# Attention of the second block's layers: values in column strips, outputs summed turned in PSUM, paired scores of the second tile in 64-row tiles

## The chip, the core and the metric

The kernel runs on one core of one Trainium2 chip. All data are fp32. The metric is the device time of one execution in microseconds: three runs of the kernel before gave a median of 1697.09 us (1696.93 to 1698.31).

## The reference

Two transformer blocks in a row on 256 tokens of 1024 channels. The first block (FFN, token mixer, FFN) isn't touched. The second has two layers, and each begins with a mixer of two attentions, whose outputs stand side by side ahead of the output product:

```python
for l in range(DEPTH_2):                       # 2 layers
    h = x @ w_in[l]
    cq, ckv, kr, nq, kc, vc, ks, vs, kw, vw, gl = jnp.split(h, split_at, axis=-1)
    o_a = mla_mixer(cq, ckv, kr, ...)          # 8 heads, 64 value columns each, causal
    o_b = nsa_mixer(nq, kc, vc, ks, vs, kw, vw, gl, ...)
    mix = jnp.concatenate([o_a, o_b], axis=-1) @ w_out[l]
    x = layer_norm(DEEPNORM_ALPHA * x + mix, ln1_g[l], ln1_b[l])
    ...                                        # memory attention, conv FFN
# nsa_mixer, for a block of 128 queries, 8 heads in 2 groups of 4 that share keys and values:
#   o_c: softmax over 15 compressed keys;  o_s: selected keys;  o_w: window keys
    return gi[..., 0:1] * o_c + gi[..., 1:2] * o_s + gi[..., 2:3] * o_w
```

With 256 tokens the selection and the window take in every earlier key, so o_s and o_w are two causal attentions with their own keys and values. `gi` are sigmoid gates, one for each token, head and branch.

## The kernel before

Each engine has its own program, written out by hand; the engines meet only through semaphores, so each engine's order is the order of the code. An attention is a list of units (`UNITS_2`), and a unit is a pair of heads (index `s`) for one tile of 128 queries. The kinds in question are K (all eight heads on the compressed keys), S (selected), W (window) and M (latent attention, `mla_mixer`). A tile has four units each of S, W and M, numbered `n`. In tile 0 a unit has 128 keys, in tile 1 it has 256. The order is K of tile 0, K of tile 1, then for each tile S0, W0, S1, W1, S2, W2, S3, W3, M0 to M3: 26 units.

A unit goes through a pipeline, with unit j at its scores while older units are behind:
- TensorE `scores(j)` (L1190): a 128x128 product for each head, into one half of `PS` (L1187). The keys of S and W are 64 channels in 128 rows, padded with zeros.
- VectorE `logits(j)` (L2357): adds the bias, takes the row maximum, and negates it (L2360).
- ScalarE `exps(j)` (L1692): exponential with row sums.
- TensorE `turn(j-2)` (L1206): transposes the probabilities, two blocks of 128 in tile 0, four in tile 1.
- ScalarE `out_of_psum(j-2)` (L1702): copies them into `PTS`, which has two buffers. Unit j's copy waits until the values of unit j-2 are done (`values_ready`, L1699). In each step of ScalarE's program this copy stands ahead of `exps(j)`.
- TensorE `value(j-3)` (L1232): the transposed probabilities are the weights (128 columns), the values move (64 columns), the outputs have tokens in the partitions.
- VectorE `output(j-3)`: reciprocal of the sums (L2403), for S and W times the gate (L2413), and scales the output out of PSUM into `O1`, S and W added onto what is there (L2419); M is written (L2421), K too, over 512 columns (L2408).

The M unit's bias is the causal mask alone. For K, `logits` is a memset and three small steps (L2338 to L2346), and `mid` masks the probabilities and sums them (L2371 to L2375). `mid(j)` on VectorE, between logits and output, does something only for kinds with `mid` set: here K.

A fp32 matmul appears as two passes in the trace, a transpose as one. Between the first steps stand four pieces of the memory values' product (L1538, eight passes of 512 columns each; TensorE's table `between`, L1556).

Behind the attention `shared_product` multiplies by `w_out` (L844). It needs the mix turned, channels in the partitions, in `XT`. TensorE turns `O1` in four batches of four transposes (L1116), two for each tile, and ScalarE copies each batch out (L1603, L1609). The first product blocks need only tile 0; later ones need sums of weights and of both tiles' activations, which VectorE makes after the attention (`weight_sums` L2191 to L2203, `act_sums` L2217 to L2223).

## Time and profile before

| what | value |
|---|---|
| median of three runs | 1697.09 us |
| profiled execution | 1696.81 us, its span 1694.9 us |
| TensorE busy (matmul) | 1665.5 us, 98% |
| VectorE busy | 1223.2 us, 72% |
| ScalarE busy | 352.5 us, 21% |
| chain that ended last | PE 90%, DVE 5% |

The span is what the profile covers; the device time is about 1.9 us longer. In the rows PE is TensorE's matmuls, PEld its weight loads, DVE is VectorE, ACT is ScalarE. The layers' attention stands at 831 to 892 us (layer 0) and again 481 us later (layer 1). A matmul's busy time includes the tail of its pipeline, so passes overlap in the rows; what one costs the next is read from the distance of the starts.

### The profile page before, as it was taken

What the parts mean: (1) busy time and instruction counts of PE and PEld (TensorE: products, weight loads), DVE (VectorE), ACT (ScalarE), POOL (GpSimd) and SP (SyncE); (2) the same over time, 40 slices, a digit from 0 to 9 for tenths busy, and PEclk for the clock granted to TensorE, in tenths of its full rate; (3) what the DMA queues carried; (4) which work ended last, traced back from release to release, by engine and by line L of the source; (5) the groups of instructions that cost most, each with busy time, mean ns of one, the idle gap of its engine ahead of it and who ended that gap; (6) DMA issues with size and microseconds to landing.
All of it is one profiled execution on the core that took longest, in us unless ns stands there. A gap on an engine that the chain in (4) does not pass through costs nothing.

```text
span 1694.9 us, 22817 instructions
## 1 busy us (share of the span) xinstructions
PE 1665.5 (98%) x8726; PEld 1281.4 (76%) x8726; DVE 1223.2 (72%) x2230; ACT 352.5 (21%) x893; POOL 212.7 (13%) x139
## 2 busy tenths in 40 slices
PE   7999999999999999999999999999999999999998
PEld 6887488877847886477784969994687767699953
DVE  6777467976787777573376778996844685789995
ACT  2111000034511111112270212220012531222210
POOL 1222211121021212211001000002120000000021
PEclk9999999999999999999999999999999999999999
DMA  9685454524176555346513536444447206265440
GB/s 320 194 230 177 146 199 162 175 80 149 51 232 213 160 164 184 124 145 178 207 51 131 155 125 194 156 170 153 158 121 252 100 1 224 71 226 177 150 173 25
DMA packets 163755, 267.07 MB, mean 158 GB/s; under 512 B 4279, under 2 KB 106477, under 8 KB 163519
## 3 DMA queue, kind: packets, MB, share of 16 engines
q1 hardware_dynamic: 157902, 248.66, 43.8%
q0 software_dynamic: 5008, 15.91, 3.3%
q8 instruction: 70, 1.15, 0.3%
q10 hardware_dynamic: 736, 1.05, 0.3%
q14 instruction: 39, 0.31, 0.1%
HBM read 262.52 MB, written 2.03 MB: 156 GB/s over the span
## 4 chain that ended last, share of the span: by engine, by line
PE 90%; DVE 5%; DVEq 2%; issue 1%; ACT 1%; DMA 1%; SPq 0%; ACTq 0%
PE psum L1017 19%; PE psum L886 16%; PE psum L1065 13%; PE psum L952 12%; PE psum L844 7%; PE psum L1275 4%; PE psum L1481 3%; PE psum L1538 3%; PE psum L1190 3%; PE psum L1116 3%; PE psum L1232 2%; PE psum L825 2%; PE psum L1104 2%; PE psum L1206 1%; PE psum L1221 1%
## 5 line engine op out<-in xcount | busy, mean ns | idle before, releaser
L695 POOL TENSOR_TENSOR work<-ring,work 128x1024 f32<-128x1024 f32 (+2 forms) x59 | 147.4, 2499 | 791.5 <-DVE work L2199 791.5
L2191 DVE TENSOR_TENSOR work<-ring 128x1024 f32<-128x1024 f32 (+2 forms) x102 | 122.0, 1196 | 83.3 <-PE psum L1065 74.3
L1065 PE MATMUL psum<-ring,work 128*128 128x512 f32 x352 | 160.8, 592 | 0.0
L2195 DVE TENSOR_TENSOR ring<-ring 128x1024 f32<-128x1024 f32 (+2 forms) x104 | 131.7, 1267 | 7.7
L2199 DVE TENSOR_TENSOR work<-ring 128x1024 f32<-128x1024 f32 (+2 forms) x102 | 122.6, 1202 | 7.6
L1065 PEld LDWEIGHTS psum<-ring,work 128*128 128x128 f32 x352 | 66.4, 190 | 81.1 <-issue 79.9
L1065 PE MATMUL psum<-work 128*128 128x512 f32 x264 | 122.5, 592 | 0.0
L1017 PE MATMUL psum<-x_t,work 128*128 128x128 f32 x832 | 101.4, 275 | 0.0
L1017 PE MATMUL psum<-work,ring 128*128 128x128 f32 x832 | 101.4, 275 | 0.0
L1017 PE MATMUL psum<-x_t,ring 128*128 128x128 f32 x832 | 97.4, 275 | 1.6 <-ACT x_t L1610 1.6
L1017 PEld LDWEIGHTS psum<-x_t,work 128*128 128x128 f32 x832 | 97.1, 192 | 0.0
L1017 PEld LDWEIGHTS psum<-work,ring 128*128 128x128 f32 x832 | 97.1, 192 | 0.0
L1017 PEld LDWEIGHTS psum<-x_t,ring 128*128 128x128 f32 x832 | 95.0, 192 | 2.4 <-issue 2.4
L1065 PEld LDWEIGHTS psum<-work 128*128 128x128 f32 x264 | 49.7, 190 | 62.0 <-issue 60.3
L2823 DVE SCALAR_TENSOR_TENSOR work<-work 128x254 f32<-128x254 f32 (+1 forms) x176 | 83.5, 526 | 3.3
L886 PE MATMUL psum<-ring,work 128*128 128x256 f32 x352 | 83.2, 379 | 0.0
L886 PE MATMUL psum<-ring,x_t 128*128 128x256 f32 x352 | 81.7, 386 | 1.5 <-DMA ring<-in_ffn_w_gate_dram 1.3
L886 PE MATMUL psum<-work,x_t 128*128 128x256 f32 x352 | 82.9, 379 | 0.0
L1190 PE MATMUL psum<-work 128*128 128x256 f32 (+2 forms) x384 | 79.5, 338 | 0.3 <-DVE stat L2360 0.3
L886 PEld LDWEIGHTS psum<-ring,x_t 128*128 128x128 f32 x352 | 67.9, 194 | 12.2 <-DMA ring<-in_ffn_w_gate_dram 2.4
L1692 ACT ACTIVATE work<-work,stat 128x256 f32<-128x256 f32 (+1 forms) x136 | 61.6, 453 | 66.5 <-DVE stat L2360 65.6
L886 PEld LDWEIGHTS psum<-ring,work 128*128 128x128 f32 x352 | 66.9, 190 | 9.1
(304 smaller groups left out, 2865.6 us busy)
## 6 DMA issues: line engine op xcount, KB each, us to landing
ring<-in_ffn_w_up_dram SPq DMA_DIRECT2D x66, 1024.0 KB, 7.9
ring<-in_w_in_dram SPq DMA_DIRECT2D x21, 2048.0 KB, 7.9
ring<-in_ffn_w_down_dram SPq DMA_DIRECT2D x20, 2048.0 KB, 7.8
ring<-in_ffn_w_gate_dram SPq DMA_DIRECT2D x22, 1024.0 KB, 5.7
ring<-in_xa_wkv_dram SPq DMA_DIRECT2D x8, 2048.0 KB, 9.5
ring<-in_w_out_dram SPq DMA_DIRECT2D x6, 2048.0 KB, 10.9
ring<-in_xa_wq_dram SPq DMA_DIRECT2D x4, 2048.0 KB, 7.9
ring<-in_xa_wo_dram SPq DMA_DIRECT2D x4, 2048.0 KB, 11.3
```

The costliest lines, as they stand in the source:

```text
L695: nc.gpsimd.tensor_tensor(t4, quarters(n, chunks, pitch)[2], t2, ALU.subtract).then_inc(fourth_ready, 1)
L844: last = mm(share_bank(p), acts[p][:, q, :], rhs[:, i, :], start=(q == 0), stop=(q == KD // 2 - 1))
L886: last = mm(corners(j)[p], acts[p][:, i, :], rhs[:, i, :], start=(i == 0), stop=(i == KD // 2 - 1))
L952: last = mm(row_corners(j)[p][:, 0:pitch // 2], acts[p][:, i, :], rhs[:, i, :], start=(i == 0), stop=(i == KD // 2 - 1))
L1017: last = mm(corners(j)[p][:, c * P:(c + 1) * P], weights[:, i, c * P:(c + 1) * P], acts[p][:, i, :], start=(i == 0), stop=(i == KD // 2 - 1))
L1065: last = mm(sums[p], acts[p][:, q, :], rhs[:, i, :], start=(q == 0), stop=(q == KF // 2 - 1))
L1190: last = mm(PS[:, o:o + x["keys"]], q, k[:, 0:x["keys"]], start=(c == 0), stop=(c == len(pairs) - 1))
L1275: last = mm(row_corners(q + 1)[p], acts_of_gates[p][:, i, :], rhs[:, i, :], start=(i == 0), stop=(i == KD // 2 - 1))
L2191: v.tensor_tensor(t3, b22, b12, ALU.subtract)
L2195: v.tensor_tensor(b12, b12, b11, ALU.subtract)
L2199: v.tensor_tensor(t2, b22, b12, ALU.subtract).then_inc(forms_ready, 1)
L2823: last = v.scalar_tensor_tensor(dst, UP[:, q, 0:T - t], CWT[:, 2 - t, k:k + 1], dst, ALU.mult, ALU.add)
```

## The change

- K of tile 1 moves in the list from the second place to the head of tile 1's units.
- Values of S, W and M: the values are now the weights (64 columns) and the transposed probabilities move (128 columns). The two heads of a pair go to PSUM partitions 0 to 63 and 64 to 127, that is to two column strips of the array. Two units are done in one block behind the second of them (`turned_values`): S with W, M0 with M1, M2 with M3. K's values are four products with 128 columns.
- The outputs come out turned, and K, S and W of a tile are summed in one PSUM bank (`PO[:, 0:512]`), M in the other.
- Since the sum is taken in PSUM, the softmax's reciprocal and the gate are multiplied into the probabilities ahead of the transposes: S, W and M now have `mid` work on VectorE, K has more of it, and `output` does nothing for these kinds.
- ScalarE copies a tile's sum straight into `XT` (`turned_rows_out`). The turning of the mix ahead of the output product and its copies are gone.
- S and W scores of tile 1 use 64 rows of the array for each head (no zero rows) and are issued together for S and W (`scores_by_rows`), with the two heads in different PSUM banks (pitch 512).

```diff
@@ -227,15 +227,17 @@
     keys = T if kind == "X" else 2 * NC if kind == "K" else P * (tile + 1)
     subs = 3 if kind == "A" else 4 if kind == "K" else 2
 
-    return dict(kind=kind, n=n, tile=tile, keys=keys, subs=subs, pitch=512 if kind == "C" else keys, nk=1 if kind == "K" else keys // P,
-                wide=kind == "A", mid=kind in "BKX")
+    return dict(kind=kind, n=n, tile=tile, keys=keys, subs=subs, pitch=512 if kind == "C" or kind in "SW" and tile else keys, nk=1 if kind == "K" else keys // P,
+                wide=kind == "A", mid=kind in "BKSWMX")
 
 
 UNITS_1 = [unit("B", h, i) for i in range(TT) for h in range(4)] + \
           [unit("A", h, i) for i in range(TT) for h in range(4)] + \
           [unit("C", h, i) for i in range(TT) for h in range(2)]
-UNITS_2 = [unit("K", 0, i) for i in range(TT)] + \
-          [x for i in range(TT) for x in [unit(k, h, i) for h in range(4) for k in "SW"] + [unit("M", h, i) for h in range(4)]]
+UNITS_2 = [x for i in range(TT) for x in
+           [unit("K", 0, i)] + [unit(k, h, i) for h in range(4) for k in "SW"] + [unit("M", h, i) for h in range(4)]]
+SPARSE_UNITS, TILE_UNITS = 9, 13
+assert len(UNITS_2) == TT * TILE_UNITS
 UNITS_X = [unit("X", h, i) for i in range(TT) for h in range(2)]
 U1, U2 = len(UNITS_1), len(UNITS_2) + len(UNITS_X)
 LAST_B, LAST_A = (max(j for j, x in enumerate(UNITS_1) if x["kind"] == k) for k in "BA")
...
@@ -1123,6 +1125,8 @@
             def half_turned(b0, c, l=None):
                 if b0 == "X":
                     pe.wait_ge(unit_done, at(U1 + len(UNITS_2) + c + 1, U2, l))
+                elif b0 == "O":
+                    pe.wait_ge(unit_done, at(U1 + TILE_UNITS * (1 + c // 2), U2, l))
                 else:
                     pe.wait_ge(turned_out, at(b0 + c + 1, B_LAYER, l))
 
...
@@ -1179,8 +1181,25 @@
+                def scores_by_rows(j):
+                    u = u0 + j
+                    pe.wait_ge(group_free, at(H_WV + 2, G_LAYER, l))
+                    pe.wait_ge(logits_ready, at(u, U2, l))
+                    for t in (j, j + 1):
+                        x = units[t]
+                        for s in range(2):
+                            r = slice(HD * s, HD * s + HD)
+                            o = ((u0 + t) % 2) * 1024 + s * x["pitch"]
+                            (q, k), = query(x, s, 1)
+                            last = mm(PS[:, o:o + x["keys"]], q[r], k[r, 0:x["keys"]], start=True, stop=True)
+                        last.then_inc(scores_ready, 1)
+
+                    if x["kind"] in "SW" and x["tile"]:
+                        if x["kind"] == "S":
+                            scores_by_rows(j)
+                        return
...
@@ -1207,13 +1226,41 @@
+                def turned_values(j):
+                    x, u = units[j], u0 + j
+                    k = x["kind"]
+                    if k == "K":
+                        if x["tile"]:
+                            pe.wait_ge(unit_done, at(U1 + SPARSE_UNITS, U2, l))
+                        for c in range(4):
+                            last = mm(PO[:, c * P:(c + 1) * P], VBD[:, c // 2, (c % 2) * P:(c % 2 + 1) * P],
+                                      PTS[:, u % 2, (c // 2) * P:(c // 2 + 1) * P], start=(c == 0), stop=False)
+                        last.then_inc(values_ready, 1)
+                        return
+                    if k == "M" and x["tile"] and x["n"] == 1:
+                        pe.wait_ge(unit_done, at(U1 + TILE_UNITS, U2, l))
+                    for t in (j - 1, j):
+                        y = units[t]
+                        o = (512 if k == "M" else 0) + P * y["n"]
+                        for kb in range(y["nk"]):
+                            for s in range(2):
+                                n = s * y["nk"] + kb
+                                last = mm(PO[HD * s:HD * s + HD, o:o + P], values(y, s, kb), PTS[:, (u0 + t) % 2, n * P:(n + 1) * P],
+                                          start=(k == "M" and y["n"] == 0 and kb == 0), stop=(y["kind"] != "S" and y["n"] == 3 and kb == y["nk"] - 1))
+                    last.then_inc(values_ready, 2)
+
+                    k = x["kind"]
+                    if k == "S" or k == "M" and x["n"] % 2 == 0:
+                        return
+                    if k in "KWM":
+                        turned_values(j)
+                        return
...
@@ -1437,15 +1484,6 @@
-                def turn_mixed(b0, units, ready, l):
-                    def turn(i):
-                        if i == 0:
-                            pe.wait_ge(unit_done, at(units, U2, l))
-                            turn_rows(b0, O1, None, l, None, [0])
-                        else:
-                            turn_rows(b0, O1, ready, l, None, [1])
-                    return turn
-
...
@@ -1555,7 +1593,7 @@
-                shared_product(L_OUT, F_LOUT + F_LAYER * l, A_LOUT + A_LAYER * l, E_O, turn_mixed(E_O, U1 + TT + 12, 19, l), l)
+                shared_product(L_OUT, F_LOUT + F_LAYER * l, A_LOUT + A_LAYER * l, "O", lambda i: None, l)
...
@@ -1713,6 +1751,19 @@
+                def turned_rows_out(j):
+                    x, u = units[j], u0 + j
+                    act.wait_ge(values_ready, at(u + 1, U2, l))
+                    i, sparse = x["tile"], x["kind"] == "W"
+                    src = PO[:, 0:512] if sparse else PO[:, 512:1024]
+                    src = src.rearrange("p (k t) -> p k t", k=4)
+                    dst = XT[:, 4:8, i * P:(i + 1) * P] if sparse else XT[:, 0:4, i * P:(i + 1) * P]
+                    if not sparse and i == 0:
+                        copy(dst[:, 0:2, :], src[:, 0:2, :]).then_inc(quarter_out, 1)
+                        copy(dst[:, 2:4, :], src[:, 2:4, :]).then_inc(unit_done, TILE_UNITS - SPARSE_UNITS)
+                    else:
+                        copy(dst, src).then_inc(unit_done, SPARSE_UNITS if sparse else TILE_UNITS - SPARSE_UNITS)
+
...
@@ -1725,6 +1776,8 @@
+                    if 0 <= j - 3 < n and units[j - 3]["kind"] in "WM" and units[j - 3]["n"] == 3:
+                        turned_rows_out(j - 3)
...
@@ -1936,7 +1989,6 @@
-                turned_rows(E_O, XT, l)
...
@@ -2368,16 +2420,26 @@
-                        v.tensor_tensor(L3, L3, cmp_ok[:, x["tile"], :, :], ALU.mult).then_inc(mixed_ready, 1)
+                        v.tensor_tensor(L3, L3, cmp_ok[:, x["tile"], :, :], ALU.mult)
+                        dr()
+                        v.reciprocal(RC[:, b4, :], SM[:, b4, :])
+                        dr()
+                        v.tensor_tensor(RC[:, b4, :], RC[:, b4, :], ngate[:, x["tile"], 0::3], ALU.mult)
+                        dr()
+                        v.tensor_tensor(L3, L3, RC[:, b4, :, None].to_broadcast([P, 8, NC]), ALU.mult).then_inc(mixed_ready, 1)
-                    if x["kind"] == "X":
+                    if x["kind"] in "SW":
+                        c = 3 * 2 * x["n"] + (1 if x["kind"] == "S" else 2)
+                        v.tensor_tensor(RC[:, b4, 0:2], RC[:, b4, 0:2], ngate[:, x["tile"], c:c + 4:3], ALU.mult)
+                        dr()
+                    if x["kind"] in "SWMX":
...
@@ -2392,33 +2454,19 @@
-                    if k == "X":
+                    if k in "KSWMX":
-                    m = 1 if k == "A" else 8 if k == "K" else 2
+                    m = 1 if k == "A" else 2
-                    if k == "K":
-                        v.tensor_tensor(RC[:, b4, :], RC[:, b4, :], ngate[:, i, 0::3], ALU.mult)
-                        dr()
-                        v.tensor_tensor(O1[:, i, 512:1024].rearrange("p (h e) -> p h e", h=8), o.rearrange("p (h e) -> p h e", h=8),
-                                        RC[:, b4, :, None].to_broadcast([P, 8, HD]), ALU.mult).then_inc(unit_done, 1)
-                        return
-                    if k in "SW":
-                        c = 3 * 2 * n + (1 if k == "S" else 2)
-                        v.tensor_tensor(RC[:, b4, 0:2], RC[:, b4, 0:2], ngate[:, i, c:c + 4:3], ALU.mult)
-                        dr()
-                        c = {"A": n * HD, "C": 768 + (2 * n + s) * HD, "M": (2 * n + s) * HD}.get(k, 512 + (2 * n + s) * HD)
-                        dst = O1[:, i, c:c + HD]
-                        if k in "SW":
-                            last = v.scalar_tensor_tensor(dst, o[:, s * HD:(s + 1) * HD], RC[:, b4, s:s + 1], dst, ALU.mult, ALU.add)
-                        else:
-                            last = v.tensor_scalar(dst, o[:, s * HD:(s + 1) * HD], RC[:, b4, s:s + 1], None, ALU.mult)
+                        c = {"A": n * HD, "C": 768 + (2 * n + s) * HD}[k]
+                        last = v.tensor_scalar(O1[:, i, c:c + HD], o[:, s * HD:(s + 1) * HD], RC[:, b4, s:s + 1], None, ALU.mult)
...
@@ -2791,7 +2839,7 @@
-                act_sums_of(at(E_O + 4, B_LAYER, l))
+                act_sums_of(at(U1 + len(UNITS_2), U2, l), unit_done)
```

TensorE, first tile, from one value block to the next, before (L1232 values, L1190 scores, L1206 transposes):

```order
L1232 MATMUL psum<-work 128x64 [waits unit_done,probs_out]
L1232 MATMUL psum<-work 128x64
L1190 MATMUL psum<-work 128x128 [waits logits_ready]
L1190 MATMUL psum<-work 128x128
L1206 MATMUL psum<-ident_fours,work 128x128 [waits probs_out,probs_ready]
L1206 MATMUL psum<-ident_fours,work 128x128
```

The same place after (L1209 scores, L1225 transposes, L1248 values of two units in strips of 64 columns):

```order
L1209 MATMUL psum<-work 128x128 [waits logits_ready]
L1209 MATMUL psum<-work 128x128
L1225 MATMUL psum<-ident_fours,work 128x128 [waits probs_out,mixed_ready]
L1225 MATMUL psum<-ident_fours,work 128x128
L1248 MATMUL psum<-work 64x128 [waits probs_out]
L1248 MATMUL psum<-work 64x128 x3
L1209 MATMUL psum<-work 128x128 [waits logits_ready]
L1209 MATMUL psum<-work 128x128
L1225 MATMUL psum<-ident_fours,work 128x128 [waits probs_out,mixed_ready]
L1225 MATMUL psum<-ident_fours,work 128x128
```

One value block stands for two units, and scores and transposes of the next units stand ahead of and behind it; transposes wait for `mixed_ready`, from VectorE's `mid`, where they waited for `probs_ready`, from ScalarE.

TensorE, second tile, a unit of S or W before:

```order
L1190 MATMUL psum<-work 128x256 [waits logits_ready]
L1190 MATMUL psum<-work 128x256
L1206 MATMUL psum<-ident_fours,work 128x128 [waits probs_out,probs_ready]
L1206 MATMUL psum<-ident_fours,work 128x128 x3
L1232 MATMUL psum<-work 128x64 [waits unit_done,probs_out]
L1232 MATMUL psum<-work 128x64 x3
```

A pair of S and W after (L1194 scores in 64-row tiles, L1225 transposes, L1248 values):

```order
L1194 MATMUL psum<-work 128x256 [waits logits_ready,group_free]
L1194 MATMUL psum<-work 128x256 x3
L1225 MATMUL psum<-ident_fours,work 128x128 [waits probs_out,mixed_ready]
L1225 MATMUL psum<-ident_fours,work 128x128 x3
L1248 MATMUL psum<-work 64x128 [waits probs_out]
L1248 MATMUL psum<-work 64x128 x7
L1225 MATMUL psum<-ident_fours,work 128x128 [waits probs_out,mixed_ready]
L1225 MATMUL psum<-ident_fours,work 128x128 x3
```

Both units' scores stand ahead of the first unit's transposes, and the values of the pair before between the two units' transposes.

VectorE, first tile, a W or S unit before (L2357 and L2360 logits, L2403 to L2419 output of an older unit):

```order
L2357 ISA work,stat<-psum,work 128x128 [waits probs_turned,scores_ready]
L2357 ISA stat 128x1
L2357 ISA work,stat<-psum,work 128x128
L2357 ISA stat 128x1
L2360 TENSOR_SCALAR stat<-stat 128x2
L2403 RECIPROCAL stat<-stat 128x2 [waits values_ready]
L2413 TENSOR_TENSOR stat<-stat,work 128x2
L2419 SCALAR_TENSOR_TENSOR work<-psum,stat,work 128x64 x2
```

The same place after (L2409 and L2412 logits, L2436 to L2444 `mid` of the unit before):

```order
L2409 ISA work,stat<-psum,work 128x128 [waits probs_turned,scores_ready]
L2409 ISA stat 128x1
L2409 ISA work,stat<-psum,work 128x128
L2409 ISA stat 128x1
L2412 TENSOR_SCALAR stat<-stat 128x2
L2436 RECIPROCAL stat<-stat 128x2 [waits probs_ready]
L2440 TENSOR_TENSOR stat<-stat,work 128x2
L2444 TENSOR_SCALAR work<-work,stat 128x128 x2
```

The scaling waits for the exponentials (`probs_ready`) and works on 128 keys for each head, where it waited for the values and worked on 64 columns.

## Rows read from the trace of the kernel before

**Rows 1.** Page, part 2: granted TensorE clock in 40 slices of the span.

```profile
PEclk9999999999999999999999999999999999999999
```

**Rows 2.** Second tile: length; busy us of PE, PEld, DVE, ACT, POOL; clock; DMA.

```profile
864.00:886.00 22.00, 22.00 (x158) 20.12 (x158) 18.17 (x101) 17.75 (x60) 0.00 (x0) 1.00 0.00 1
```

**Rows 3.** Timeline of TensorE, front and first tile: start, us, line, operands, count.

```profile
832.38 3.70 PE L1538 MATMUL psum<-ring,work 128*128 128x512 f32 x8 [0.30 <-ACT work L1905]
...
851.89 0.66 PE L1190 MATMUL psum<-work 128*128 128x128 f32 x4
...
863.78 1.08 PE L1190 MATMUL psum<-work 128*128 128x256 f32 x4
```

**Rows 4.** Timeline, second tile and output product: TensorE, and one VectorE row.

```profile
885.00 0.60 PE L1206 MATMUL psum<-ident_fours,work 128*128 128x128 f32 x4
885.44 1.00 PE L1232 MATMUL psum<-work 128*128 128x64 f32 x8
886.28 1.08 PE L1190 MATMUL psum<-work 128*128 128x256 f32 x4
887.20 0.60 PE L1206 MATMUL psum<-ident_fours,work 128*128 128x128 f32 x4
...
891.98 1.04 PE L1116 MATMUL psum<-ident_fours,work 128*128 128x128 f32 x8
893.15 3.67 PE L844 MATMUL psum<-ring,x_t 128*128 128x512 f32 x8
...
899.18 0.69 DVE L2219 TENSOR_TENSOR work<-work,x_t 128x512 f32<-128x512 f32 x1
```

**Rows 5.** Timeline of TensorE around the compressor's products in 32-column strips.

```profile
800.86 1.03 PE L1481 MATMUL psum<-work,ring 128*128 128x256 f32 x4
...
801.82 1.95 PE L1493 MATMUL psum<-ring,work 128*32 128x128 f32 x64
803.70 0.70 PE L1481 MATMUL psum<-work,ring 128*128 128x256 f32 x2
```

**Rows 6.** Timeline of TensorE around two index scores in 64-row tiles.

```profile
385.60 0.70 PE L1337 MATMUL psum<-work 64*128 64x256 f32 x4
386.24 0.66 PE L1116 MATMUL psum<-ident_fours,work 128*128 128x128 f32 x4
```

**Rows 7.** Timeline of VectorE, a unit of each tile.

```profile
852.16 0.28 DVE L2357 CUSTOM_DVE_ANT_0 work<-psum,work 128x128 f32<-128x128 f32 x1
...
872.42 0.41 DVE L2357 CUSTOM_DVE_ANT_0 work<-psum,work 128x256 f32<-128x256 f32 x1
...
873.34 0.16 DVE L2403 RECIPROCAL stat<-stat 128x2 f32<-128x2 f32 x1
873.57 0.16 DVE L2413 TENSOR_TENSOR stat<-stat,work 128x2 f32<-128x2 f32 x1
```

**Rows 8.** Scaling of probabilities in other attentions, and TensorE waiting for it.

```profile
L2387 DVE TENSOR_SCALAR work<-work,stat x8: 286/320/355, 412.9 to 430.8; 128x128 f32<-128x128 f32 x4, 128x256 f32<-128x256 f32 x4
...
964.09 0.62 DVE L2382 TENSOR_SCALAR work<-work,stat 128x256 f32<-128x256 f32 x2
...
964.76 0.66 PE L1206 MATMUL psum<-ident_fours,work 128*128 128x128 f32 x4 [0.15 <-DVE work L2382]
```

**Rows 9.** Timeline of ScalarE: exponentials of a unit; two copies in a row.

```profile
873.46 0.51 ACT L1692 ACTIVATE work<-work,stat 128x256 f32<-128x256 f32 x1 [0.22 <-DVE stat L2360]
...
874.37 0.19 ACT L1692 ACTIVATION_READ_ACCUMULATOR work<-work,stat 128x1 f32 x1
...
971.63 0.59 ACT L1714 COPY x_t<-psum 128x512 f32<-128x512 f32 x1 [1.09 <-PE psum L1221]
972.12 0.59 ACT L1702 COPY work<-psum 128x512 f32<-128x512 f32 x1
```

**Rows 10.** Timeline of VectorE in a K unit's logits.

```profile
832.20 0.27 DVE L2338 MEMSET work<- 128x256 f32 x1 [3.12 <-PE psum L1190]
...
833.26 0.28 DVE L2346 TENSOR_TENSOR work<-work,stat 128x120 f32<-128x120 f32 x1
```

13 lines of the change are left out of this document (5 added, 8 removed).

## The prediction

> **What bounds the kernel now.** I read the clock and the busy time first. TensorE is granted its full clock (2.4 GHz) throughout [rows 1], so nothing is to be won or lost there unless the change opens idle time. Then I read the stage that changes, which stands twice in the program (layers 0 and 1 of the second block); I work on layer 0, at 831 to 905 us, and double. In its second query tile TensorE is busy 22.0 of 22 us and the other two engines 18 each [rows 2]: TensorE sets the pace, with scores, transposes and values end to end. A unit there takes 0.92 for scores, 0.44 for four transposes and 0.84 for eight value passes, 2.20 us from one unit to the next [rows 4]. In the first tile a unit takes (863.78 - 851.89) / 8 = 1.49 us [rows 3]. Half of each of those TensorE blocks is 1.1, while VectorE's logits (0.65, below) and output (reciprocal, gate, two scalings, 0.87 in sum) make 1.5: there VectorE is the pace.
>
> **What TensorE gains, block by block.** In a strip the weights are 64 value columns and the moving part 128 columns. No 64-column strip is in the trace. The nearest is the compressor's product with 32-column strips: 64 passes in 1.95 us, 0.03 each, where full-width passes of 128 columns take 0.44 / 4 = 0.11 [rows 5, 4]. So strips run side by side, and I put two at 0.055 a pass: eight passes 0.44, a pair of second-tile units with 16 passes 0.87 instead of 1.68. Entering strips is not free: the four passes ahead of the compressor end at 801.89, each 0.38 long and 0.216 apart, so the next could have started at 801.73 and started at 801.82: 0.09. Leaving costs 0.11, and the first weight load is in the open, since two full passes then take 0.70 instead of 0.60 [rows 5]. I take 0.09 a change, plus the open load: 0.05 for 64 columns or a transpose, 0.11 for 128. The bounds are 0 (load and change hidden) and 0.20 a change.
>
> Two 64-row scores are 4 passes, and the next block starts 0.64 us later [rows 6], against 0.92. Two units in one block come to 0.64 + 0.44 = 1.08 for 1.84 before. Added up, a second-tile pair of S and W needs 1.2 + 0.98 + 1.0 = 3.2 us of TensorE, against 4.4. That is the gain on paper, and it has a rule behind it and one against it. The Trainium skill (TensorEngine Tiling (Array Packing), Performance Considerations) recommends exchanging the moving and the stationary operand for a free dimension of 64 and up to 2x from it; the compressor's passes agree. The same page (Key Properties) states that changing the tiling mode drains the TensorE. The 0.09 above agrees in kind; a literal drain of the 0.27 us pass would be 0.16 a change, some 2 us more over both layers than my sum.
>
> **What the change puts on the other engines.** Before, an S, W or M unit went from exponentials straight to the transposes, and its scaling followed behind the values, off the path. Now the scaling (reciprocal, gate product, two products over the keys) stands between exponentials and transposes. Reciprocal to gate product is 0.23, and I take the same for the gate product [rows 7]; two scalings of 256 elements take 0.62 [rows 8]: 1.09 us, on VectorE, in the path. One of 128 elements takes 0.286 against 0.35 at 256 [rows 8], so the pair is 0.49 and the step 0.96 (bounds 0.85 and 1.09). VectorE's own load hardly changes: 0.92 + 1.09 - 0.06 = 1.95 for a second-tile unit (before 1.81), 1.55 for one of the first tile.
>
> **The new wait.** The values of a pair are now one block behind the second unit, and both PTS buffers belong to that block. ScalarE's copy of the next pair's S unit waits for it, and the exponentials of the pair after that are queued behind the copy. That closes a loop. Second tile, S and W: scaling 1.09, to TensorE 0.05 [rows 8], transposes 0.44 + 0.05 (0.44 from [rows 4]), values 0.09 + 0.05 + 0.87, tail of the last pass 0.16 (0.60 - 0.44 in [rows 4]) and handover 0.04, copy 0.48, exponentials 873.46 to 874.56 = 1.10 [rows 9], handover 0.03. Sum 4.45 us a pair, where TensorE took 4.39: the 1.2 us of TensorE's gain becomes waiting.
>
> First tile, S and W: the W unit's scores stand behind the values, and S's scaling behind W's logits, so the loop is scaling 0.96 + 0.05, transposes 0.27, values 0.09 + 0.05 + 0.44, scores 0.09 + 0.11 + 0.44, tail and handover 0.20, logits 0.65 (0.92, less 0.13 for each of the two shorter steps [rows 7]): 3.35 a pair, where 3.0 was enough. M units have no gate product: 3.11 a pair. M in the second tile, same kind of loop: scaling 0.85 + 0.05, transposes 0.49, values 1.01, scores 0.09 + 0.11 + 0.87, tail and handover 0.20, logits 0.92: 4.59.
>
> **Sum for a layer**, as lateness against before.
> 1. Front: one K unit leaves the stretch in which memory values hide it. TensorE's order is K, chunk, S, chunk, W and turn, chunk, S, turn, K values, chunk, W, turn, S. From 832.38 with chunks of 3.5 and 3.44 [rows 3], scores 0.44, turns 0.22 and K values 0.87, the third S unit starts at 849.5, before 851.9: -2.4.
> 2. From there to the second tile's first scores: 2 x 3.35 + 2 x 3.11 = 12.9, and the K unit, now amid the stream: logits 1.34, in steps of 0.35 [rows 10], and in `mid` three such steps and three of 0.23, 1.7, together 3.1 on VectorE. 16.0 against 11.9: +4.1.
> 3. To the last M unit's scores, 5.5 pairs: 4 x 4.45 + 1.5 x 4.59 = 24.7, against 886.28 - 863.78 = 22.5: +2.2.
> 4. Drain: last scores 0.97, tail 0.20, logits 1.03, exponentials 1.10, scaling 0.85, transposes 0.49, tail 0.20, copy 0.59, values 0.92, handovers 0.17, and 0.35 because two copies stand ahead on ScalarE: 6.9, against 891.98 - 886.28 = 5.7: +1.2.
> 5. The mix's transposes go: 891.98 to 893.15 becomes 0.1, -1.1, and the second batch of eight, -0.9 [rows 4]. ScalarE's copies behind them go with them. Late next could be VectorE's sums for that product. Before, its scaling ended and the weight sums began 1.1 us after the last values, and the second activation sum was there at 899.87, 7.9 after them [rows 4]. Now VectorE is free at the end of the last scaling, 2.2 ahead of the end of the last values, so that sum is there 7.9 - 3.3 = 4.6 after them; TensorE wants it after two products over 6.9 us (each eight passes, like the one at 893.15). Covered: 0.
> 6. At three seams (S/W to M, M to K, K to S/W) a unit starts before the loop behind it closes: -0.1 each, my estimate.
>
> -2.4 + 4.1 + 2.2 + 1.2 - 2.0 - 0.3 = +2.8 us a layer. Two layers +5.6. The profiled execution took 1696.81 us around its span of 1694.9; with the change 1702.4. The median of the three runs is 0.3 above the profiled one: 1702.7.
>
> **Rivals.**
> Faster: the loop doesn't bind, because the handovers overlap more than I think, and VectorE alone is the pace: 1.95 for S and W, 1.72 for M, against 2.20 before. That gives -(8 x 0.25 + 4 x 0.48) = -3.9 in the second tile; with +0.7 for K, +0.2 for the first tile, +1.2 for the drain and -2.0 for the transposes it is -3.8 a layer, 1689.5. For it speaks that the TensorE blocks do shrink; against it, that each link of the loop is a wait in the code. Chance 0.11.
> No change: mode changes and weight loads are hidden and a 128-element scaling is nearer 0.22. That takes 0.25 off each of the ten pairs that a loop paces, 2.5 a layer: 1697.7. Against it are the 0.09 and 0.10 of [rows 5]. Chance 0.16.
> Slower by more, one mechanism: 64-column strips don't run side by side (a change that doesn't do what it says). Then a pair's values cost 0.44 more in the first tile and 0.87 in the second, 4 x 0.44 + 6 x 0.87 = 7 a layer, 1717. It decides as soon as a value pass costs over 0.07. Against it stand the 0.03 us of [rows 5]. Chance 0.05.
> Clock: TensorE's busy share in the stage falls to some 0.6. If its clock fell to 1.2 GHz there, the TensorE links of the loops double (about 1.5 a pair in ten pairs), +30 us, 1733. No stretch of the trace shows a fall, but none idles so much [rows 1]. Chance 0.02.
> Forecast (the loops as summed): 0.66.
>
> **Numbers.** 1702.7 us. The forecast's own spread is 1700 to 1706 (the bounds on mode changes, scaling and handovers, about 1 to 1.5 us a layer). Taking in the no-change case the range is 1696.5 to 1706.5; it leaves out the faster case and the two dear ones. A measurement of this kernel tells 0.2%, 3.4 us, from no change: 1693.7 to 1700.5. Slower: the forecast but for a tenth of it, and the dear cases, 0.67. Within: no change and the rest, 0.20. Faster: 0.13.
>
> **What would show it.** In the profile after, TensorE's share in the attention windows falls from full to about two thirds while their length grows; ScalarE's copies wait for value passes, by over 1 us in every other unit; the pair takes 4.4 to 4.5 us in the second tile and 3.3 to 3.4 in the first; 16 strip passes take 0.9 to 1.0 us; the K unit of tile 1 holds VectorE 3 us; the output product starts right behind the last values and 2 to 4 us later than before. A pair at 3.9 us in the second tile would make the loop wrong, and with it the forecast; an unchanged length of the first tile would put the error on the mode changes.

## The result: 11 us slower, twice the loss forecast, and the profile after

The changed kernel takes 1708.14 us (median of five runs, 1707.77 to 1708.73), the kernel before 1697.09 beside it: ratio 1.0065, 95% interval 1.0051 to 1.0079. The forecast was 1702.7 us, with a range of 1696.5 to 1706.5. The sign was right; 5.6 us of loss were forecast and 11.0 came, so the time lies 1.6 us above the range. The span went from 1694.9 to 1706.3 us. One execution of e10 below ran in a slow state (2169 us, mean clock 0.751), and since it is the one that was profiled, nothing is read from e10's trace.

The page's shares hardly move, and its row of clocks is the one of [rows 1]: a fall of a few us doesn't show in a slice of 43 us. So [rows 1] could not show what the prediction read from it, a full clock throughout. In the kernel before itself the clock is at 0.50 for the last 5.2 us of the span, where TensorE has no work left, and the last slice still reads nine:

```profile
1689.70:1694.90 5.20, 0.00 (x0) 0.00 (x0) 2.63 (x4) 0.20 (x1) 0.00 (x0) 0.50 0.54 202
```

Every kernel here ends like that; below, "no fall" is said of the attention's stage in the profiled execution. One has to ask for short stretches. These are of the kernel after, in the columns of [rows 2] (length; busy us and instructions of PE, PEld, DVE, ACT, POOL; clock; DMA share; GB/s): four pieces of the stage, then the whole stage in layers 0 and 1, from the first scores to the output product.

```profile
866.00:870.10 4.10, 2.12 (x20) 1.37 (x19) 3.32 (x18) 1.45 (x6) 0.00 (x0) 1.00 0.00 0
870.10:873.50 3.40, 3.40 (x19) 2.32 (x15) 2.66 (x14) 1.89 (x7) 0.00 (x0) 0.50 0.01 2
873.50:877.00 3.50, 3.17 (x26) 2.39 (x27) 2.72 (x15) 3.04 (x10) 0.00 (x0) 1.00 0.02 5
1354.80:1361.60 6.80, 6.39 (x31) 4.91 (x32) 4.70 (x24) 3.45 (x12) 0.00 (x0) 0.50 0.00 0
831.24:898.91 67.67, 55.19 (x382) 37.78 (x380) 43.75 (x232) 37.06 (x131) 0.00 (x0) 0.97 0.18 63
1317.11:1385.45 68.34, 56.49 (x381) 38.91 (x379) 43.34 (x232) 37.19 (x131) 0.00 (x0) 0.95 0.18 62
```

The clock is 0.50, 1.2 GHz, for 3.4 us in layer 0 and for 6.8 us in layer 1, and 1.00, 2.4 GHz, around them. What TensorE did before it fell is in its timeline, of layer 0 (start, us, line, operation, operands, count, idle time and what ended it):

```profile
865.82 1.14 PE L1194 MATMUL psum<-work 64*128 64x256 f32 x8 [0.41 <-DVE work L2398]
866.88 0.44 PE L1225 MATMUL psum<-ident_fours,work 128*128 128x128 f32 x2
869.30 0.44 PE L1225 MATMUL psum<-ident_fours,work 128*128 128x128 f32 x2 [1.98 <-DVE work L2433]
869.67 0.76 PE L1248 MATMUL psum<-work 128*64 128x128 f32 x8
870.36 2.08 PE L1194 MATMUL psum<-work 64*128 64x256 f32 x8
872.37 1.11 PE L1225 MATMUL psum<-ident_fours,work 128*128 128x128 f32 x4
873.27 1.17 PE L1236 MATMUL psum<-work 128*128 128x128 f32 x8
874.28 0.60 PE L1225 MATMUL psum<-ident_fours,work 128*128 128x128 f32 x4
874.81 1.13 PE L1194 MATMUL psum<-work 64*128 64x256 f32 x8
...
879.22 1.13 PE L1194 MATMUL psum<-work 64*128 64x256 f32 x8 [0.36 <-DVE stat L2412]
```

TensorE waits 1.98 us for the K unit's last product on VectorE (L2433), and soon after it four paired scores (L1194) take 2.08 us where they take 1.13 a pair later, four transposes 1.11 for 0.60. In layer 1 there is the same wait, 1.98 us up to 1355.21, and the fall begins inside it, at 1354.8. The pair of units goes from 874.81 to 879.22, 4.41 us; 16 strip passes (L1248) start at 885.94 and the next scores at 886.96, 1.02 later. ScalarE in that stretch:

```profile
878.05 0.59 ACT L1740 COPY work<-psum 128x512 f32<-128x512 f32 x1 [1.50 <-PE psum L1248]
...
879.53 0.57 ACT L1740 COPY work<-psum 128x512 f32<-128x512 f32 x1
...
882.59 0.59 ACT L1740 COPY work<-psum 128x512 f32<-128x512 f32 x1 [1.50 <-PE psum L1248]
```

Every other copy waits 1.50 us for a value block, and the two that wait are 4.54 us apart: the loop of the forecast, summed at 4.45. And the end of the stage, again TensorE's timeline, beside the last units of [rows 4]:

```profile
885.35 0.66 PE L1225 MATMUL psum<-ident_fours,work 128*128 128x128 f32 x4 [1.09 <-DVE work L2444]
885.94 1.09 PE L1248 MATMUL psum<-work 128*64 128x128 f32 x16
886.96 1.13 PE L1209 MATMUL psum<-work 128*128 128x256 f32 x4
...
891.58 1.13 PE L1209 MATMUL psum<-work 128*128 128x256 f32 x4
892.54 0.60 PE L1225 MATMUL psum<-ident_fours,work 128*128 128x128 f32 x4
894.94 0.66 PE L1225 MATMUL psum<-ident_fours,work 128*128 128x128 f32 x4 [1.79 <-DVE work L2444]
895.53 1.09 PE L1248 MATMUL psum<-work 128*64 128x128 f32 x16
896.55 0.66 PE L1225 MATMUL psum<-ident_fours,work 128*128 128x128 f32 x4
897.88 1.09 PE L1248 MATMUL psum<-work 128*64 128x128 f32 x16 [0.68 <-ACT work L1740]
898.91 1.12 PE L846 MATMUL psum<-ring,x_t 128*128 128x512 f32 x2
```

The M pair is 886.96 to 891.58, 4.62; the product starts right behind the last strips, at 898.91 for 893.15 before.

### The profile page after: what moved, and what is told of

It reads as the page before. It is cut to its first block, busy times and chain, and to the rows that moved or that the text cites. A ratio compares the mean times of both kernels' runs of the same rounds, so it can differ in the third digit from the quotient of the medians.

```text
span 1706.3 us, 22755 instructions
## 1 busy us (share of the span) xinstructions
PE 1653.9 (97%) x8710; PEld 1258.6 (74%) x8710; DVE 1225.0 (72%) x2230; ACT 349.6 (20%) x893; POOL 212.5 (12%) x139
## 3 DMA queue, kind: packets, MB, share of 16 engines
q8 instruction: 69, 1.13, 0.3%
## 4 chain that ended last, share of the span: by engine, by line
PE 81%; DVE 12%; DVEq 3%; issue 2%; ACT 1%; DMA 1%; SPq 0%; ACTq 0%
PE psum L888 15%; PE psum L1067 13%; PE psum L1019 12%; PE psum L954 11%; PE psum L846 6%; PE psum L1322 3%; PE psum L1519 3%; PE psum L1576 3%; PE psum L1118 2%; PE psum L1209 2%; PE psum L827 2%; PE psum L1106 2%; PE psum L1225 1%; DVE work L2871 1%; DVE ring L2247 1%
## 5 line engine op out<-in xcount | busy, mean ns | idle before, releaser
L1067 PEld LDWEIGHTS psum<-ring,work 128*128 128x128 f32 x352 | 66.3, 190 | 81.8 <-issue 79.9
L888 PEld LDWEIGHTS psum<-ring,work 128*128 128x128 f32 x352 | 66.9, 190 | 9.1
L1641 ACT ACTIVATE work<-psum 128x512 f32<-128x512 f32 (+4 forms) x66 | 34.7, 550 | 180.6 <-PE psum L1118 180.3
```

The lines of the kernel that those rows point to most:

```text
L888: last = mm(corners(j)[p], acts[p][:, i, :], rhs[:, i, :], start=(i == 0), stop=(i == KD // 2 - 1))
L1067: last = mm(sums[p], acts[p][:, q, :], rhs[:, i, :], start=(q == 0), stop=(q == KF // 2 - 1))
```

## The experiments

Each kernel ran five times or more between runs of the kernel before on the same chip; ratios are to that one. "The stage" is the time from its first scores to the output product: 60.9 us in both layers of the kernel before, plus 2.0 us for the mix's transposes (1.17 ahead of the product, 0.85 within it), which the change removes. So a kernel built on the change is level with before at 62.9.

**e1, the paired scores alone.** In the kernel before:

```diff
+                    if x["kind"] in "SW" and x["tile"]:
+                        if x["kind"] == "S":
+                            scores_by_rows(j)
+                        return
```

> The kernel before, with the second tile's S and W scores issued in pairs of 64-row passes and nothing else changed. My theory (the change loses by the scaling in the path, the late K unit and the loop over the two PTS buffers, not by the paired scores): in the second tile TensorE needs 0.64 + 4 x 0.44 / 2 + 2 x 0.84 = 3.2 us a pair where it took 4.39; now the pair waits for both logits, and the loop is logits 0.92, the older unit's output 0.87, logits 0.92, scores and handovers 1.1: 3.8 us. Four pairs a layer by 0.55, two layers: 4.5 us faster, ratio 0.997, about 1692.5. Rival: the wait for both logits of the pair eats the gain or more, and part of the change's loss is here: ratio 1.000 to 1.003.

1702.17 us (1699.59 to 1705.82), ratio 1.0034 (1.0022 to 1.0047): slower; the rival's direction was right, and the time is above its 1.003. TensorE's timeline of e1 (L1192 paired scores, L1223 turn, L1249 values):

```profile
863.07 0.64 PE L1249 MATMUL psum<-work 128*128 128x64 f32 x4
865.00 2.08 PE L1192 MATMUL psum<-work 64*128 64x256 f32 x8 [1.29 <-DVE stat L2377]
...
874.22 1.14 PE L1192 MATMUL psum<-work 64*128 64x256 f32 x8 [0.44 <-DVE stat L2377]
...
877.06 1.00 PE L1249 MATMUL psum<-work 128*128 128x64 f32 x8
878.85 1.14 PE L1192 MATMUL psum<-work 64*128 64x256 f32 x8 [0.78 <-DVE stat L2377]
```

The pair waits for both logits (L2377); the second logits stand on VectorE behind the older unit's output, and that behind the values. This pair takes 4.63 us, not 3.8; the four of layer 0 take 5.28, 3.94, 4.63 and 3.68, together 17.5 us where the kernel before has 15.9 from its first second-tile scores to its first M scores (863.78 to 879.69). And the clock is at 1.2 GHz for 3.4 us in either layer, from 864.9 in layer 0, at the end of a wait of only 1.29 us. The five executions differ with their mean granted clock: 1699.59 us at 0.999, three of 1702.1 to 1702.4 at 0.997, 1705.82 at 0.994. By the first of these the waiting alone costs about 3 us against the 1696.63 of the kernel before, and the falls the rest.

**e2, the strips alone.** The changed kernel without the four lines above, and with the pitch of before.

> The changed kernel, with the second tile's scores issued unit by unit in full mode as before (the strips, the scaling ahead of the turn, the K unit's place stay). My theory: a pair of the second tile is paced by the loop scaling, turn, values, copy, exponentials at 4.4, and TensorE's 2 x 0.92 + 0.98 + 1.0 = 3.8 fits in it, so the pair stays at 4.4 and the time within 1 us of the changed kernel's, ratio 1.006; if the busier TensorE keeps its clock at 2.4 GHz after the K unit, 1 to 3 us less, ratio 1.0045 to 1.006. Rival (TensorE's blocks are on the loop after all): pair at 4.8 or more, 3 to 6 us more than the changed kernel, ratio 1.008 to 1.010.

1707.69 us, ratio 1.0072 (1.0059 to 1.0084). No fall. Two of the five executions took 1710.2 and 1710.8 us, at a mean clock of 0.998 and 0.997 for 0.999 in the others; the trace is of one of the others. The stage is 68.0 and 67.8 us. A second-tile pair takes 4.85, as the rival had it (scores start at 877.43 and 882.28), so TensorE's blocks were on the loop after all; the time came out as mine only because the fall was gone. Read with e6, the two answers separate.

**e3, TensorE kept busy in the K unit's wait.** The changed kernel with, ahead of the turn of the second tile's K unit:

```diff
+                    if x["kind"] == "K" and x["tile"]:
+                        pe.wait_ge(probs_out, at(u - 1, U2, l))
+                        for _ in range(14):
+                            nc.tensor.transpose(PT[:, (u % 2) * 512:(u % 2) * 512 + P], ident, ident)
```

> The changed kernel, with 14 transposes of no use (0.11 us each, 1.5 us) put into the 1.98 us in which TensorE waits for the K unit of the second tile. Clock theory (the fall to 1.2 GHz for 3.4 us in layer 0 and 6.8 us in layer 1 behind that wait costs about 1 and 2 us): no stretch at 1.2 GHz, TensorE's blocks behind the wait at their usual length, 2.5 to 3.5 us faster than the changed kernel, ratio 1.0045 to 1.005. Rival (VectorE and ScalarE pace the stretch, and the clock costs nothing): the clock may stay up but the time is that of the changed kernel, ratio 1.0065.

1705.47 us, ratio 1.0053 (1.0041 to 1.0066). Layer 1 has no fall and its stage went from 68.34 to 66.33 us. In layer 0 the fall came 25 us later, at 894.7, behind the drain's wait of 1.79 us. That is the profiled execution, 1706.41 us; the other four took 1705.3 to 1705.5.

**e6, both waits filled.** As e3, with 9 transposes ahead of the turn of the third M unit too.

> As e3, with 9 more transposes of no use in the second wait of over 1 us that the changed kernel has, ahead of the turn of the second tile's third M unit: in e3 the fall of layer 0 went from the K unit's wait to there. Clock theory: no stretch at 1.2 GHz at all, both layers 66.3 us from the first scores to the output product as layer 1 in e3, so 1.3 + 2.0 = 3.3 us faster than the changed kernel: 1704.3, ratio 1.0045. Rival: the fall comes somewhere else again, ratio 1.005 to 1.006.

1705.44 us, ratio 1.0049 (1.0037 to 1.0062). The windows of the stage in e6:

```profile
831.44:898.38 66.94, 56.47 (x404) 39.44 (x402) 43.43 (x232) 37.12 (x131) 0.00 (x0) 1.00 0.18 64
1316.56:1382.89 66.33, 56.44 (x404) 39.44 (x402) 42.91 (x232) 37.11 (x131) 0.00 (x0) 1.00 0.18 65
```

No fall, with 23 passes of no use a layer. The time is between theory and rival, and no better than e3's median: the second filling clears the profiled execution of its fall and wins nothing that the medians show. So the falls cost 67.67 - 66.94 = 0.7 in layer 0 and 68.34 - 66.33 = 2.0 in layer 1, 2.7 us together. The ratios differ by 0.16%, 2.7 us as well, though with intervals of 0.13% on either side; but no execution of the changed kernel is under 1707.77 (mean clock 0.996 to 0.997), and none of e6 over 1705.59 (0.998 to 0.999). At an unbroken 2.4 GHz the paired scores gain 68.0 - 66.9 = 1.1 and 67.8 - 66.3 = 1.4 over e2: in the change as made the falls took that back. The S and W pairs of the second tile in e6 (layer 0):

```profile
870.53 1.13 PE L1194 MATMUL psum<-work 64*128 64x256 f32 x8
...
874.70 1.13 PE L1194 MATMUL psum<-work 64*128 64x256 f32 x8 [0.37 <-DVE stat L2416]
...
878.55 1.13 PE L1194 MATMUL psum<-work 64*128 64x256 f32 x8 [0.37 <-DVE stat L2416]
...
882.72 1.03 PE L1209 MATMUL psum<-work 128*128 128x256 f32 x4
```

They take 4.17, 3.85 and 4.17 us, not 4.41 as in the change as made, where the fall stands just ahead.

**e4, four buffers for the turned weights.**

```diff
-                    if j >= 2:
-                        act.wait_ge(values_ready, at(u - 1, U2, l))
+                    late = 4 if x["kind"] in "KSWM" else 2
+                    if j >= late:
+                        act.wait_ge(values_ready, at(u + 1 - late, U2, l))
```

> The changed kernel with four buffers for the turned weights instead of two, so that ScalarE's copies wait for the values of two pairs back. Loop theory: the S and W pair of the second tile falls from 4.4 to VectorE's 2 x 1.95 = 3.9, the M pair from 4.6 to 3.5, the first tile's pairs from 3.37 to 3.1; 4 x 0.5 + 1.5 x 1.1 + 4 x 0.25 = 4.6 a layer, 9 us in both: 1699, ratio 1.001. Rival (VectorE, or the chain of one unit, is the pace and the buffers only look like it): pairs unchanged, ratio 1.0065.

1704.31 us, ratio 1.0047 (1.0033 to 1.0061), with 6.8 us at 1.2 GHz still in layer 1. In layer 0, without a fall, the stage is 65.4, 1.5 less than in e6. TensorE's timeline there (L1197 paired scores, L1228 turn, L1251 strips, L1212 M scores):

```profile
874.20 1.13 PE L1197 MATMUL psum<-work 64*128 64x256 f32 x8 [0.37 <-DVE stat L2416]
...
878.05 1.14 PE L1197 MATMUL psum<-work 64*128 64x256 f32 x8 [0.36 <-DVE stat L2416]
...
881.37 0.81 PE L1212 MATMUL psum<-work 128*128 128x256 f32 x3
```

S and W pairs take 3.85 and 3.32 us. The 3.85 is e6's too, with two buffers; what the buffers win comes behind it, 3.32 for 4.17 and 3.05 for 3.73 from the first M scores to the second. VectorE waits 0.75 and 0.58 us for exponentials there in e6 and never over 0.25 us in e4, so the buffers were that loop. The first tile's pairs (3.37) and the last M pair (4.6) did not move; my expectation was wrong there and the forecast right, since its loops for them have no copy in them but scores behind values.

**e5, the scaling out of the path.** The turn is released by the reciprocal, and the scaling's work follows it into a spare buffer; the kernel leaves out the scaling of the S, W and M weights.

```diff
+                        v.reciprocal(RC[:, b4, 0:2], SM[:, b4, 0:2]).then_inc(mixed_ready, 1)
...
+                            v.tensor_scalar(spare[:, s * n:(s + 1) * n], L[:, s * n:(s + 1) * n], RC[:, b4, s:s + 1], None, ALU.mult)
```

> The changed kernel, with VectorE's scaling of the S, W and M weights left out of the path but not out of VectorE's load: TensorE's turn is released by the reciprocal, 0.16 us, and the gate product and the two products over the keys follow, at their usual length, into a buffer that nobody reads (so the outputs are not scaled). Theory of the path: the pairs lose the scaling's 0.8 to 1.1 us twice over what VectorE's load allows: second tile S and W from 4.4 to 3.9, M from 4.6 to 3.7, first tile from 3.37 to 3.1, the drain 0.7 shorter; 4 x 0.5 + 1.5 x 0.9 + 4 x 0.27 + 0.7 = 5.1 a layer: 10 us faster than the changed kernel, 1698, ratio 1.0005. Rival (VectorE's load is the pace, whatever stands in the path): under 2 us, ratio 1.0055 or more.

1700.04 us, ratio 1.0016 (1.0008 to 1.0025). VectorE has nearly the same load (busy 42.3 us in the stage of layer 0 for 43.8), and the stage is 63.7 and 63.8 us, with falls of 6.8 and 3.4 us still in it, 3.9 and 4.5 less than in the changed kernel. That is the path, not the load. The fall of layer 0 begins at 865.4, ahead of the K unit's wait and behind one of only 0.89 us:

```profile
864.85 1.60 PE L1194 MATMUL psum<-work 64*128 64x256 f32 x8 [0.89 <-DVE work L2398]
```

**e7, the K unit second.** The order is K, K, S, W, ... again; the second tile's K weights wait in a buffer of their own.

> The changed kernel, with the second tile's K unit back at the second place of the order (its turned weights wait in a buffer of their own for the second tile's first pair of values). My sum priced its late place at 4.1 - 0.9 = 3.2 us in the stream against 2.4 us won in front, and the wait of 1.98 us for it is where the clock falls. Theory: 4.5 us of K step go, 2.4 come back in front, 0.9 for the eight K passes in the pair that takes them stay, and the falls behind it go with the wait (0.7 and 2.0): per layer 1.2, with the clock 4.5 to 5 us faster than the changed kernel in all, 1703, ratio 1.004. Rival (the K step was only visible as a wait): ratio 1.006 or more.

1704.32 us, ratio 1.0051 (1.0038 to 1.0063), no fall in the profiled execution, of 1704.20 us; two of the five took 1707.2 and 1707.5, at a mean clock of 0.997 for 0.999. The stage is 66.4 and 66.0: against e6 only 0.6 and 0.3 less, for 1.2 expected; the rest of its gain is the falls. The late K unit costs little by itself; in the changed kernel's trace its wait is what the clock falls behind, but by the two slower executions an early K unit doesn't rule a fall out.

**e8, paired scores in the kernel before, with VectorE's order mended.**

```diff
+                    if j < n and paired != "W":
+                        logits(j)
+                    if paired == "S":
+                        dve.wait_ge(probs_ready, at(u0 + j - 2, U2, l))
+                        factors(j - 3)
+                        logits(j + 1)
```

> The kernel before with paired scores in the second tile, but for the first pair, and with VectorE's order mended for them: the logits of both units of a pair one behind the other, with the reciprocal and the gate product of the older unit between them, and only then the older unit's output. In e1 a pair took 4.63 us, since the second unit's logits stood behind the older unit's output, and that behind the values; and the first pair waited 1.29 us for both logits, behind which the clock fell to 1.2 GHz. Theory: three pairs a layer at VectorE's 2 x (0.95 + 0.9) = 3.7 in place of 4.39: 4 us faster than before, 1692.5, ratio 0.9976. Rival (TensorE again waits at each pair's start, or the clock falls): ratio 1.000 or more.

1695.89 us, ratio 0.9994 (0.9985 to 1.0003): no difference that can be told. The pairs take 3.43 to 3.78 us, 3.7 expected, but ahead of the first TensorE waits 1.33 us for both logits, with no fall behind it, and the stage is 60.5 for 60.9 us. The 4 us that I expected did not come.

**e9 and e10, scores one place ahead.**

```diff
+                    if early <= j < n - 1:
+                        scores(j + 1)
                     if 0 <= j - 2 < n:
                         turn(j - 2)
```

> The changed kernel with four buffers for the turned weights, as e4, and TensorE's scores of each unit (behind the first five) issued one place earlier: ahead of the turn of three units back, not behind it and the values. e4 opened the loop over the buffers (S and W pair of the second tile 4.2 to 3.85 and 3.3 us), but the other loops of the forecast, in which scores stand behind values, stayed: 3.37 in the first tile, 4.6 for an M pair of the second. Theory: with both open VectorE is the pace, 3.1 and 3.0 in the first tile, 3.9 and 3.5 in the second: 5 x 0.27 + 1.5 x 1.1 = 3.0 a layer better than e4, 1698.5, ratio 1.001. Rival (one unit's own chain, not the order of the blocks, is the pace): ratio as e4, 1.0045.

> e9 and the K unit at the second place, as e7. Theory: e7 is 66.2 us from the first scores to the output product, four buffers take 1.5 off (e4 against e6 in layer 0), the scores ahead 2.5 to 3, and no stretch falls to 1.2 GHz: 62 us where before has 60.9 and 2.0 of transposes more, so -0.9 a layer: 1695, ratio 0.999 (0.997 to 1.0005). Rival: VectorE, with the scaling of 128 and 256 keys a head in its load, is slower than TensorE was before, and what the loops cost comes back as its load: ratio 1.0015 or more.

e9 took 1712.16 us, ratio 1.0089 (1.0075 to 1.0103); e10 1705.81, ratio 1.0052 (1.0039 to 1.0066). Both are misses, and e10's is not explained by a trace. In e9 the first tile did as expected (scores at 855.67 and 858.72, 3.05 a pair), but the second did not:

```profile
864.60 2.08 PE L1197 MATMUL psum<-work 64*128 64x256 f32 x8 [1.72 <-DVE work L2405]
...
871.20 2.08 PE L1197 MATMUL psum<-work 64*128 64x256 f32 x8 [2.23 <-DVE stat L2419]
...
883.17 1.13 PE L1197 MATMUL psum<-work 64*128 64x256 f32 x8 [2.05 <-DVE stat L2419]
```

A pair issued early waits for two logits ahead of a turn that is ready, and in layer 0 alone the clock is at 1.2 GHz for 13.7 and 3.4 us; layer 1 adds 3.4 twice.

**e11 and e12, the same with that mended.** e11 keeps the pairs at their own place and issues only unpaired scores ahead; e12 has no pairs. Both have the four buffers and the early K unit.

```diff
+                steps = [t - (t > 5 and n > 20 and not (x["tile"] and x["kind"] in "SW")) for t, x in enumerate(units)]
```

> e10 with the paired scores of the second tile back at their own place (in e9 the pair issued one place early waited for both logits ahead of a turn that was ready, three waits of 1.7 to 2.2 us in layer 0, and 17 us at 1.2 GHz); the unpaired scores stay one place ahead, four buffers and the early K unit stay. Theory: the first tile at 3.05 a pair as e9 had it, the second as e4 with M pairs at 3.9: from e7's 66.2 down 1.5 for the buffers, 1.3 for the first tile, 1.0 for M: 62.4 us, where parity is at 62.9: 1697, ratio 0.9995 to 1.001. Rival: the pair's wait for both logits leaves idle time in which the clock falls again, ratio 1.002 or more.

> The same with the second tile's scores unit by unit, all of them one place ahead: strips, four buffers, early K unit, no pairs. Theory: nothing on TensorE waits for two logits, VectorE paces both tiles (3.1 and 3.0 a pair in the first, 3.9 and 3.5 in the second), TensorE's 3.8 fits just in: 62.5 to 63.5 us from the first scores to the output product, 1697 to 1699, ratio 1.000 to 1.001, no fall. Rival: TensorE's 3.8 us of a pair and VectorE's 3.9 don't overlap fully and the pair takes 4.2 or more: ratio 1.002 or more.

e11: 1693.12 us, ratio 0.9979 (0.9971 to 0.9988); e12: 1694.02, ratio 0.9984 (0.9975 to 0.9993). Both are faster than the kernel before, and than the changed kernel by 15 and 14 us. Both came out better than expected (1697, and 1697 to 1699), and neither rival's ratio came; the stage of e11 is 60.7 and 60.2 us where 62.4 was expected, and no run says which part of the sum was too dear. The stage of layer 0 in e11, and two pairs of its second tile (L1199 pair, L1230 turn, L1242 K values, L1255 strips, L1214 M scores):

```profile
831.27:892.01 60.74, 54.20 (x381) 37.07 (x379) 42.92 (x232) 37.25 (x131) 0.00 (x0) 1.00 0.21 70
```

```profile
871.22 1.13 PE L1199 MATMUL psum<-work 64*128 64x256 f32 x8 [0.36 <-DVE stat L2422]
872.29 0.66 PE L1230 MATMUL psum<-ident_fours,work 128*128 128x128 f32 x4
872.78 1.06 PE L1242 MATMUL psum<-work 128*128 128x128 f32 x8
873.77 1.09 PE L1255 MATMUL psum<-work 128*64 128x128 f32 x16
874.79 0.66 PE L1230 MATMUL psum<-ident_fours,work 128*128 128x128 f32 x4
875.38 1.13 PE L1199 MATMUL psum<-work 64*128 64x256 f32 x8
...
878.05 1.13 PE L1214 MATMUL psum<-work 128*128 128x256 f32 x4
```

In these two pairs nothing waits over 0.4 us, in the two ahead of them nothing over 0.7, the clock stays at 2.4 GHz through the stage (a wait of 1.39 us in the drain too), and from the second tile's first scores to the last M unit's it is 19.8 us (863.58 to 883.35) for 22.5 before and 25.8 after the change.

## Why the forecast was short

The terms, in us of lateness a layer (layer 0 / layer 1), read off the timelines by the same landmarks, with e6 beside them for the change without a fall:

| step | forecast | measured | e6 |
|---|---|---|---|
| 1 front | -2.4 | -2.3 / -2.3 | -2.3 / -2.3 |
| 2 first tile with the K unit | +4.1 | +4.2 / +4.3 | +4.2 / +4.3 |
| 3 second tile | +2.2 | +3.3 / +4.2 | +2.6 / +2.2 |
| 4 drain | +1.2 | +1.6 / +1.3 | +1.6 / +1.3 |
| 5 transposes of the mix | -2.0 | -2.0 / -2.0 | -2.0 / -2.0 |
| 6 seams | -0.3 | in the steps above | |
| sum | +2.8 | +4.8 / +5.5 | +4.1 / +3.5 |

**The step that failed is the clock.** The prediction made the clock a rival with all or nothing of the stage in it (+30 us, chance 0.02) and left it out of the forecast's sum and of its spread, on the ground that no stretch of [rows 1] falls, which slices of 43 us can't tell. A small fall was open and not considered: 3.4 and 6.8 us behind the one long wait that the change makes, the K unit's 3.1 us on VectorE in the stream, which the prediction had itself summed in step 2 and priced as time alone. e6 puts the falls at 2.7 of the 5.4 us that were missed; e3, with the K unit's wait alone filled, and e7, with that wait gone, agree in direction. Without them the kernel is at 1705.4, inside the range.

**Mis-sized terms.** Without a fall 7.5 us are left where 5.6 were summed. The seams' -0.3 did not come (0.6 of the 1.9); the drain was 7.3 and 7.0 for 6.9; the rest is tenths in steps 1 to 3. None of these was tested alone. That step 3 comes out so near without a fall (25.0 and 24.7 us in e6 for 24.7) is partly luck: its four S and W pairs take 16.7 and 16.4 us where 4 x 4.45 = 17.8 were summed, and from the first M scores to the last it is 8.3 in both layers where 1.5 x 4.59 = 6.9 were.

**What held.** The loops, with one limit: in the first tile 3.37 us a pair for 3.35 and 3.1 for 3.11, the last M pair 4.62 for 4.59, ScalarE's waiting copies in the second tile 4.54 apart for 4.45. But the S and W pairs of the second tile are paced by that loop only in part. The 4.41 of the changed kernel stands behind the fall; in e6 they take 3.82 to 4.20 behind the first of each layer, and a pair at 3.9 was the prediction's own sign against the loop. Four pairs don't settle at one pace, and the loop's 4.45 is no figure for each of them.

Strips run side by side: 16 passes and the way out take 1.02 us, against 0.87 + 0.14 with transposes behind and 0.87 + 0.20 with scores, and eight take 0.59; so a pass costs (1.02 - 0.59) / 8 = 0.054 for 0.055. The way out is then 0.16 with the open load in it, and the way in 0.15 (four transposes and the change take 0.59, at 885.35, for 0.44): the mode changes came out near the 0.09 of [rows 5] with a load of 0.05 to 0.11, not near the 0.16 and a load of the literal drain weighed beside it from the Trainium skill (TensorEngine Tiling (Array Packing), Key Properties).

The copies wait as said. e4 and e5 show cause, not only size: opening the buffer loop takes S and W pairs to VectorE's pace, and taking the scaling out of the path alone gives 4 us a layer back. The faster case fell on this: its pace, VectorE's 3.9 a pair, needs more than two buffers (e4). Covered things stayed covered: the output product starts at once behind the values. Two signs were off: TensorE's share of the stage is 82% in layer 0 (75% from 864 to 886), not two thirds, and the product starts 5.8 us later than before, not 2 to 4.

**What e2 corrects.** The forecast said that TensorE's gain turns into waiting. Not all: without pairs a second-tile pair takes 4.85. With unpaired scores, one unit's scores stand behind the values in the way of VectorE, as in the first tile, and the pairing is worth 1.1 to 1.4 us a layer.

**Open.** 1.0 us comes behind the stage, at two places where VectorE is later by 0.4 and 0.6 us (around 1486 and 1629 us of before). Ahead of the first, one instruction on VectorE starts 0.43 us late, and the profile shows nothing that it waits for:

```profile
1489.55 0.75 DVE L2086 SCALAR_TENSOR_TENSOR x_res<-x_res,stat,work 128x512 f32<-128x512 f32 x1 [0.43 <-issue]
```

All traces read of the changed kernel and those built on it have this pause there, and e8, built on before, does not. Why it comes is not known, and the way from there to the second place wasn't followed.

## What to carry to other kernels

When a change moves a kernel from an engine that never idles to a chain of waits, price the waits twice: as time, and as what the engine's clock does around the longest of them; here falls stood at waits of 0.9 to 3.0 us. A saving on the pacing engine is only had when the order lets it be used: the same strips and pairs that lost 11 us win 3.7 us over the kernel before once two more buffers, one place in the issue order of the scores and the place of the K unit let VectorE run almost without gaps (none over 0.3 us in the second tile of e11's layer 0). Of these three only the buffers (e4) and the K unit's place (e7) were also run alone, and neither is enough: 1704.3 us each. Batching two units' work into one block makes it wait for both; ask what stands between them on the other engine.

## What the runs showed of the hardware

TensorE fell from 2.4 to 1.2 GHz at single waits, inside them or behind them: 1.98 us in both layers of the changed kernel, 1.29 us in e1, 1.79 us in e3's drain, 0.89 us in e5 and 1.7 to 3.0 us in e9. It was no rule: the drain's 1.79 us in the changed kernel itself, the K unit's 1.98 us in layer 0 of e4, e2 with waits of 1.6 and 1.8 us, and e8 with 1.33 had no fall behind them, and in e2 and e7 the mean clock says that some executions had one more than others. The same wait cost 3.4 us at 1.2 GHz in one layer and 6.8 in the other. Filling it with passes of no use paid off though they computed nothing: 23 transposes a layer made the kernel 2.7 us faster.
